# Gates of a linear recurrence in quarters of the array, its elementwise work spread and moved to VectorE, the last norm on rows of tokens

## What is computed

```
xc = causal_dwconv(x_rnn, conv_w, conv_b)            # 1280 channels, 4 taps
r = sigmoid(xb @ w_a + b_a)                          # w_a, w_x: 20 blocks of 64 x 64
i = sigmoid(xb @ w_x + b_x)
log_a = -8 * r * softplus(-lru_param)
a, mult = exp(log_a), sqrt(-expm1(2 * log_a))        # a = 0, mult = 1 where position == 0
h[t] = a[t] * h[t-1] + mult[t] * i[t] * xc[t]        # over the 512 tokens
...
x = x + gate1 * (merged @ w_out)
x = x + gate2 * ((silu(u_gate) * u_val) @ w_down)
return rmsnorm(x, final_g)                           # over the 1024 channels of each token
```

## Time and profile before

| | |
|---|---|
| median of three runs | 1829.65 us |
| the profiled execution's own time | 1828.8 us |
| its span, first to last instruction | 1827.0 us |
| PE busy | 1808.5 us (99%) |
| DVE busy | 1029.1 us (56%) |
| ACT busy | 754.9 us (41%) |
| POOL busy | 274.3 us (15%) |
| mean granted TensorE clock | 0.998 |

### The profile page before, as it was taken

The page is one execution under the profiler, slowest core; times in us unless marked ns, Lnnn a source line. Parts: engine busy times, 40 slices in busy tenths (PEclk is TensorE's granted clock), DMA queues, the critical chain, the costliest instruction groups (busy, mean ns, idle before and its releaser), DMA issues.

```text
span 1827.0 us, 21107 instructions
## 1 busy us (share of the span) xinstructions
PE 1808.5 (99%) x8268; PEld 1444.9 (79%) x8268; DVE 1029.1 (56%) x1522; ACT 754.9 (41%) x1197; POOL 274.3 (15%) x355
## 2 busy tenths in 40 slices
PE   9999999999999999999999999999999999999998
PEld 7888888878887888888887777766668888888886
DVE  8754554756566545554367587255544665435544
ACT  6554544425344222222344455355643344224431
POOL 4766536200000000000001120322110000000000
PEclk9999999999999999999999999999999999999999
DMA  6222222134235545553323222411133233323331
GB/s 213 95 84 87 70 87 90 59 114 150 93 132 179 190 150 184 191 192 96 126 81 99 92 76 76 138 64 58 35 132 122 70 98 99 92 93 92 97 99 59
DMA packets 64259, 198.92 MB, mean 109 GB/s; under 512 B 7136, under 2 KB 11488, under 8 KB 64160
## 3 DMA queue, kind: packets, MB, share of 16 engines
q1 hardware_dynamic: 64160, 197.57, 33.3%
HBM read 189.15 MB, written 8.39 MB: 108 GB/s over the span
## 4 chain that ended last, share of the span: by engine, by line
PE 71%; issue 21%; DVE 5%; ACT 1%; DMA 0%; POOL 0%; SPq 0%; POOLq 0%; DVEq 0%; ACTq 0%
PE bank L251 20%; PE bank L253 20%; PE bank L252 20%; PE bank L652 2%; DVE wlo L1396 1%; PE bank L682 1%; PE bank L667 1%; PE bank L544 1%; PE bank L297 1%; PE bank L340 1%; PE bank L356 1%; DVE tile L1932 1%; PE bank L386 0%; PE bank L377 0%; ACT whi L831 0%
## 5 line engine op out<-in xcount | busy, mean ns | idle before, releaser
L251 PE MATMUL bank<-tiler,whi 128*128 128x512 f32 x2260 | 909.1, 402 | 4.5 <-DVE tiler L1423 1.2
L253 PE MATMUL bank<-tiler,wlo 128*128 128x512 f32 x2260 | 891.8, 395 | 0.0
L252 PE MATMUL bank<-tiler,whi 128*128 128x512 f32 x2260 | 891.4, 394 | 0.0
L831 ACT ACTIVATE whi<-raw 128x1024 fp32r<-128x1024 f32 x284 | 298.8, 1054 | 559.1 <-PE bank L253 552.8
L251 PEld LDWEIGHTS bank<-tiler,whi 128*128 128x128 f32 x2260 | 426.1, 189 | 114.0 <-issue 14.5
L253 PEld LDWEIGHTS bank<-tiler,wlo 128*128 128x128 f32 x2260 | 425.5, 188 | 99.6
L252 PEld LDWEIGHTS bank<-tiler,whi 128*128 128x128 f32 x2260 | 426.1, 189 | 96.6 <-issue 3.3
L1396 DVE TENSOR_TENSOR wlo<-raw,whi 128x1024 fp32r<-128x1024 f32 x263 | 325.0, 1240 | 274.8 <-ACT whi L831 274.5
L2187 POOL TENSOR_TENSOR stat<-stat,scl 128x4 f32<-128x4 f32 x7 | 7.5, 1079 | 1120.3 <-DVE stat L1414 693.1
L2126 DVE SCALAR_TENSOR_TENSOR tile<-bank,sm,tile 128x511 f32<-128x511 f32 x44 | 33.0, 750 | 97.9 <-ACT tile L1370 61.9
L2178 POOL TENSOR_TENSOR wlo<-raw,whi 128x1024 fp32r<-128x1024 f32 x21 | 49.8, 2372 | 211.0 <-ACT whi L831 211.0
(11 more groups left out here) (363 smaller groups left out, 1603.8 us busy)
## 6 DMA issues: line engine op xcount, KB each, us to landing
raw<-wst SPq DMA_DIRECT2D x284, 512.0 KB, 3.6
wide<-wadaT SPq DMA_DIRECT2D x48, 512.0 KB, 3.5
tile<-xT SPq DMA_DIRECT2D x16, 256.0 KB, 6.0
spare<-tile SPq DMA_DIRECT2D x16, 256.0 KB, 2.0
tile<-spare SPq DMA_DIRECT2D x16, 256.0 KB, 5.5
out<-tile SPq DMA_DIRECT2D x8, 256.0 KB, 2.0
tile<-gblk SPq DMA_DIRECT2D x5, 256.0 KB, 4.6
us<-tile SPq DMA_DIRECT2D x4, 256.0 KB, 2.0
```

The costliest lines, as they stand in the source:

```text
L251: e.matmul(bank, whi[:, o:o + 128], hi, start=start, stop=False)
L252: e.matmul(bank, whi[:, o:o + 128], lo, start=False, stop=False)
L253: e.matmul(bank, wlo[:, o:o + 128], hi, start=False, stop=stop).then_inc(*sig("blk", n))
L831: e.activation(whi[:, c % NHL * W:(c % NHL + 1) * W], raw[:, c % NRAW * W:(c % NRAW + 1) * W], ACT.Copy).then_inc(*sig("hi", c))
```

## The change

1. **Gates in quarters.** Each of the two products of `gate_rnn(i)` becomes two of 64 rows and 64 columns, so the blocks of zeros are no longer multiplied. The parts of `w_a` go straight (rows 0-63 to partitions 0-63 of `B[4]`, rows 64-127 to 64-127), those of `w_x` crosswise into `B[5]`, so that the four parts use the four quarters of the array. ACT reads `B[5]` back in two halves.
2. **The LRU's order.** Exponentials 0 to 4 at m = 10 and 5 to 9 at m = 14, roots at m = 15 and 16; `lru_in` for 0 to 4 at m = 11 to 13 and 5 to 9 at m = 15; `lru_x` for all ten on DVE, at m = 16 to 18; the scans at m = 18 to 21. POOL's five products are gone.
3. **The last norm on rows of tokens.** ACT also scales each `HS[m]` by the gain (`OG`, tiles 0 to 7), PE turns 128x128 pieces of them into banks 4 to 7 (first 512 channels) and 0 to 3 (last 512), ACT takes the root of the mean square and DVE its reciprocal, now one number per partition. DVE scales the four tiles of the first half, ACT the four of the second, and SP sends them in an order that alternates. POOL's power, the diagonal, the spread and the fillers are gone.

```diff
                 for c in range(2):
-                    o = i % 2 * 256 + c * 128
-                    e.matmul(B[4 + c], F(GW[i // 2])[:, o:o + 128], F(XC[i]), start=True, stop=True).then_inc(*sig("lru_g", i, c))
+                    for x in range(2):
+                        of, to = slice(64 * x, 64 * x + 64), slice(64 * (x ^ c), 64 * (x ^ c) + 64)
+                        o = i % 2 * 256 + c * 128 + 64 * x
+                        ins = e.matmul(B[4 + c][to, :], F(GW[i // 2])[of, o:o + 64], F(XC[i])[of, :], start=True, stop=True)
+                    ins.then_inc(*sig("lru_g", i, c))
...
-            busy(B[7], 5)
-            total2("fin", 64, B[6])
-            total3("fin", 66, B[6])
-            busy(B[7], 8)
-            spread("fin", 65, B[7])
+            def out_turn(half_, js, ms):
+                for j in js:
+                    if half_ and ms[0] == 4:
+                        e.wait_ge(*at("h_dn", 1, 4 + j))
+                        if j == 0:
+                            e.wait_ge(*at("root", "fin"))
+                    for m in ms:
+                        e.wait_ge(*at("gs", m))
+                        ins = e.transpose(B[(0 if half_ else 4) + j][:, m % 4 * 128:m % 4 * 128 + 128],
+                                          F(OG[m])[:, j * 128:(j + 1) * 128], ident[:, :])
+                    if ms[-1] % 4 == 3:
+                        ins.then_inc(*sig("otr", half_, j))
...
+            total2("fin", 64, sums_at)
+            out_turn(0, range(4), [0, 1])
+            total3("fin", 66, sums_at)
+            out_turn(0, range(4), [2, 3])
+            out_turn(1, range(4), [4, 5, 6, 7])
...
-                e.activation(F(XX[i]), B[5], ACT.Sigmoid, bias=col("bx", i)).then_inc(*sig("lru_i", i))
+                for x in range(2):
+                    to, of = slice(64 * x, 64 * x + 64), slice(64 - 64 * x, 128 - 64 * x)
+                    ins = e.activation(F(XX[i])[to, :], B[5][of, :], ACT.Sigmoid, bias=col("bx", i)[to, :])
+                ins.then_inc(*sig("lru_i", i))
...
-                if m == 14:
+                if m == 10:
                     for i in range(5):
                         lru_exp(i)
...
+            e.activation(st, B[0][:, 508:512], ACT.Sqrt, scale=1.0 / 1024, bias=scl[:, HALF + 1:HALF + 2]).then_inc(*sig("root", "fin"))
+            e.wait_ge(*at("inv", "fin"))
+            for j in range(4):
+                e.wait_ge(*at("otr", 1, j))
+                e.activation(F(OT[4 + j]), B[j], ACT.Copy, scale=stat[:, ST_F + j:ST_F + j + 1]).then_inc(*sig("fin_a", j))
...
-            for k in range(8):
-                e.scalar_tensor_tensor(out=F(HS[k]), in0=F(HS[k]), scalar=col("gf2", k), in1=B[7], op0=MUL, op1=MUL).then_inc(
-                    *sig("fin", k))
+            e.reciprocal(stat[:, ST_F:ST_F + 4], stat[:, ST_F:ST_F + 4]).then_inc(*sig("inv", "fin"))
+            e.wait_ge(*at("inv", "fin"))
+            for j in range(4):
+                e.wait_ge(*at("otr", 0, j))
+                e.tensor_scalar(F(OT[j]), B[4 + j], stat[:, ST_F + j:ST_F + j + 1], None, MUL).then_inc(*sig("fin", j))
...
-                if m == 18:
-                    for i in range(5, 10):
-                        e.wait_ge(*at("lru_b", i))
-                        e.wait_ge(*at("lru_q", i))
-                        e.tensor_tensor(F(XX[i]), F(XX[i]), F(XC[i]), MUL).then_inc(*sig("lru_x", i))
```

More of the change, by code:

```diff
@@ L150 @@
 ACTS2 = [(42 + 2 * m, 43 + 2 * m) for m in range(11)]
+OG, OT = range(0, 8), range(8, 16)
 CG, CU = (64, 65, 66), (67, 68, 69)
@@ L1463, in vector @@
             e.memset(ones[:, :], 1.0).then_inc(*sig("ones"))
+            e.memset(scl[:, HALF + 1:HALF + 2], 1e-6)
             e.memset(scl[:, HALF:HALF + 1], -0.5).then_inc(*sig("half"))
@@ L1961, in vector @@
                     add_up("nq", 2, 72, (30, 31))
+                if 11 <= m <= 13:
+                    for i in range(2 * (m - 11), min(2 * (m - 10), 5)):
+                        lru_in(i)
                 if m == 15:
-                    for i in range(5):
+                    for i in range(5, 10):
                         lru_in(i)
-                        if i == 0:
+                        if i == 5:
                             add_up("nk", 1, 73, (32, 33))
@@ L1968, in vector @@
                     rope_k()
-                    for i in range(5, 10):
-                        lru_in(i)
+                    for i in range(5):
+                        lru_x(i)
                 if m == 17:
@@ L1973, in vector @@
                     variance("nq", B[5], 384, ST_Q)
-                    lru_x(0)
+                    lru_x(5)
                     diagonal("nk", ST_K, 75)
-                    lru_x(1)
+                    lru_x(6)
                     diagonal("nq", ST_Q, 71)
+                    lru_x(7)
                 if m == 18:
-                    for i in range(2, 5):
+                    for i in range(8, 10):
                         lru_x(i)
+                    for i in range(2):
+                        lru_scan(i)
                 if m == 19:
                     latent("kl", 2, LAT[3:], "kg", B[6], KL)
-                    for i in range(5):
+                    for i in range(2, 5):
                         lru_scan(i)
@@ L1988, in vector @@
                     latent("ql", 3, LAT[:3], "qg", B[7], QL)
-                    for i in range(5, 10):
+                    for i in range(5, 8):
                         lru_scan(i)
-                        if i == 6:
-                            start_of("in2", 21)
                 if m == 21:
@@ L2379, in gpsimd @@
             prep(CB * NCHUNK)
-            root("fin", ST_F)
         def sync(e):
@@ L2492, in sync @@
             chunks(NCHUNK)
-            for k in range(8):
-                e.wait_ge(*at("fin", k))
-                e.dma_start(out[k], F(HS[k])).then_inc(*sig("io%d" % k, 1, by=16))
+            for k in (0, 1, 4, 2, 5, 3, 6, 7):
+                if k < 4:
+                    e.wait_ge(*at("fin", k))
+                else:
+                    e.wait_ge(*at("fin_a", k - 4))
+                e.dma_start(out[k % 4][:, k // 4 * 512:k // 4 * 512 + 512], F(OT[k])).then_inc(*sig("io%d" % k, 1, by=16))
             for k in range(8):
@@ L2611 @@
     wst = nc.dram_tensor("wst", (NCHUNK, 128, CB * 128), F32, kind="ExternalInput").ap()
-    out = nc.dram_tensor("out", (8, 128, T), F32, kind="ExternalOutput").ap()
+    out = nc.dram_tensor("out", (4, 128, 1024), F32, kind="ExternalOutput").ap()
     spare = nc.dram_tensor("spare", (8, 128, T), F32, kind="Internal").ap()
```

32 lines of the change are left out of this document (18 added, 14 removed).

## The result

| | before | after |
|---|---|---|
| median (range) | 1829.09 us (1828.51 to 1829.97, 4 runs) | 1816.78 us (1815.53 to 1818.01, 4 runs) |
| profiled execution | 1828.8 us, span 1827.0 | 1816.73 us, span 1814.9 |

The ratio is 0.9932, with a 95% interval of 0.9915 to 0.9949. A second set of five runs gave 1816.76 us and 0.9937 [0.9924, 0.9951]. The forecast was 1818.4 us; the medians differ by 12.3 us, and 11.2 had been forecast.

What follows compares the result with a forecast made beforehand. PE, busy 99% of the span, was taken to bound the kernel. Terms -5.0 - 3.5 + 0.1 - 2.8 = -11.2 us gave 1818.4 us, with a likeliest range of 1816 to 1821 and a whole range of 1815.5 to 1827.5.

Steps and rivals of the forecast that it cites:

- Gates, -5.0: Ten gate calls on PE: four quarters at once, a call 1.72 to 1.22 us, 5.0 us saved in all.
- rival (a): Gate calls: only two quarters run at a time, a call costs 2.08 us, time 1827.0; chance 0.14.
- (b): Gate calls: quarters run one after another, a call costs 3.80 us, time 1844.1; chance 0.08.
- The LRU's order, -3.5: PE's three waits for DVE and ACT in the crowded stretch go, 3.5 us back whole; bounds 0 and 3.8.
- bound of 3.8: Upper bound on the PE waits won back by the LRU's new order, forecast at 3.5 us.
- 9.3 covers 5.0 plus the 3.5 of waits: Crowded stretch: DVE has 9.3 us less, enough for PE arriving 5.0 us earlier plus its 3.5 us of waits.
- rival (d): Long DVE rows are not POOL's doing; DVE gets 1.7 us more work, waits grow by 6.7, 1828.5; chance 0.05.
- ACT at gate 9, +0.1: ACT's 12.5 us against PE's 12.2 before gate 9: on time or 0.3 late, charged 0.1 us.
- rival (c): ACT's table changes cost 1.38 us more each when both tables were recently used: 2.7 us at gate 9, 1821.2; chance 0.07.
- The end, -2.8: Last norm: first output DMA at +4.4 instead of +7.21, 2.8 us earlier, then 7.1 us to the span's end.
- upper bound of 3.1: Most the end was to gain, in us, with ACT's root taking 0.16 instead of 0.3.

Runs made afterwards that it cites:

- twice: Changed kernel with each whole gate call issued twice over; stretch from first gate to the second layer's latent product 141.45 us, from one execution.
- straight: Changed kernel with the two parts of w_x going straight, so only two quarters of the array are used; 1825.31 us, ratio 0.9981.
- order_only: Kernel before with only the LRU's new order and all its products with the root on DVE; 1824.79 us, ratio 0.9978.
- gates_only: Kernel before with only the gates in quarters; 1824.92 us, ratio 0.9975.
- pool_again: Changed kernel with lru_x for row tiles 5 to 9 back on POOL; 1816.94 us, ratio 0.9932.
- dve_scales: Changed kernel with all eight output tiles scaled on DVE and ACT's four gone; 1816.85 us, ratio 0.9929.
- best: Changed kernel with later exponentials, root on ACT and reciprocal on DVE earlier at the feed-forward norm, fewer fillers at two norms; 1817.91 us, ratio 0.9936.

## Why the prediction was right

**Gates, -5.0.** Measured alone -5.07. The call went from 1.72 or 1.73 to 1.24, where 1.22 had been put together from the earlier trace rows: 0.86 for the passes and 0.36 for entering and leaving. `twice` splits the measured call into 0.86 and 0.38. `straight` gives rival (a)'s 2.08 us when only two quarters are in use, and shows that it was the quarters that decided. Rivals (a) and (b) are out. (The kernel before has one more product on a part of the array than the text ahead of the prediction says: L418 takes 64 of the 128 rows, 12 times, one after another. It is no case of two row halves at once.)

By the Trainium skill (TensorEngine Tiling (Array Packing), Restrictions and Gotchas, Gotcha 1) different row tiles can't access one PSUM bank simultaneously. The trace disagrees for this form: in both `straight` and the changed kernel, two parts from different rows wrote bank 4 at once, each its own 64 partitions. Another page of the Trainium skill (PSUM — Partial Sum Buffer, PSUM bank collisions raise a hardware error) quotes the same rule for row tiles, but the errors that it reports for two row tiles are for writes into one bank and one quadrant (32 partitions) of it. With a rule that goes by bank and quadrant the trace agrees. Two row tiles on the same partitions of one bank were not tried.

**The LRU's order, -3.5.** Measured alone -3.98. The mechanism is as put; the size was 0.5 short and lies past the bound of 3.8 that was given. Beside `order_only`, PE lost 0.85 us at L293, 0.95 at the L251 of 1107.31 and 1.83 at L585, together 3.63 for the three waits that the profile names, and 0.35 at the L251 of 1100.77, behind another late low part. That fourth one, with 0.11 us of idle time, does not stand in the list of waits, and it is most of what was missing.

**What I held beside it and what fell.** The prediction let DVE's relief pay for an earlier PE ("9.3 covers 5.0 plus the 3.5 of waits"), and rival (d) let the waits grow by 6.7 us if it did not. `gates_only` disproves that step: the gates took 5 us less with no relief at all for DVE, and no wait grew. The 5.0 needed no cover. (d)'s first half falls too, by `pool_again`: the long rows are POOL's doing. The estimate of what they cost (5.4 us) came back as 5.3.

**ACT at gate 9, +0.1.** Measured +0.49. The rows had summed to 12.5 us for ACT against 12.2 for PE, and I took off overlaps of 0.1 a row. From the start of gate 7's sigmoid to the end of gate 8's ACT took 1034.03 - 1021.19 = 12.84 us. The term was mis-sized by 0.4, past the 0.3 named as its worst. That it offsets most of the 0.5 by which the one before was short is luck. Table loads took 1.28 us and the next instruction began 0.02 us or less behind, as in the earlier trace rows; rival (c) is out. The Trainium skill (ScalarE: Activation LUTs, What ACT_TABLE_LOAD costs) gives 2.66 us with a drain for each change of table; the trace disagrees here, with 1.28 us and no drain to be seen.

**The end, -2.8.** Measured -2.92. Step by step from the last L254: sums at +0.24 as said, root at +3.00 for 3.1 (2.9, and 0.2 until the sums are visible), lasting 0.26 for 0.3, reciprocal 0.18 for 0.2, first DMA +4.29 for 4.4. The upper bound of 3.1 does not follow from the root of 0.16 that it names, which gives 2.9 to 3.0; nothing hangs on it. Then 7.02 us for 7.1: `dve_scales` shows that the bytes and not the engines set it.

**What was not in the sum.** -0.43 us ahead of the first gate, where nothing was changed, and -0.13 in two other stretches. The 0.43 arise in the first 50 us, and at that place the thirteen profiles spread from 0.8 us earlier to 1.4 later than before: that part is chance. Forecast -11.2; measured -12.1 between the two profiled executions and -12.3 between the medians.

## What to carry to other kernels

Products whose weights are two 64x64 blocks on a diagonal are worth laying in four quarters, crosswise in a second bank, if the passes that fall away take more than the 0.38 us that a visit to the split array cost here. Put several such products into one visit, since the price is paid once for each. Where engines follow each other by one chunk, as here, a shortening ahead of a crowded stretch moved the whole crowd and was kept in full. So run a term alone before a cover is subtracted from it. And count what a stretch costs from the starts of its instructions: the waits named in the profile, with 0.17 us added to each, fell 0.5 us short of the 4.0 that the stretch gave back.

## What the runs showed of the hardware that was not expected

The clock is lost for a moment in every profile at the layer's input norm, where PE does one-column sums and fillers: it falls to half (1.2 GHz) some time after 947 us, for 3.4 us in ten of the profiles and for 6.8 in three (`straight`, `dve_scales`, `best`). From the same matmul near 932 us to the first gate the ten took 40.5 to 40.6 us, `straight` and `dve_scales` 42.2, and `best`, with 3 fillers for 10, 40.9. That is one part of why executions of one kernel differ by 1 to 3 us, and the profiles show two more. `best` lost 1.8 us ahead of the norm, with a stretch at half clock near 9 us. `gates_only` and `twice` lost 1.6 us evenly between about 560 and 950 us, at a granted clock of 1.00 and where nothing was changed; the cause is open, and it is why their first gates start at 974.3 us where eight others start at 972.0 to 973.1. `dve_scales` has the long stretch with all 10 fillers in place, so whether `best` had it for its 3 is open.

POOL and DVE lengthen each other at more places than the one predicted. In the changed kernel, POOL's product `i * xc` of row tile 9 and then DVE's rows at that time:

```profile
1038.93 1.74 POOL L2407 TENSOR_TENSOR tile<-tile 128x512 f32<-128x512 f32 x1 [3.55 <-ACT tile L1170]
```

```profile
1038.22 0.69 DVE L1956 SCALAR_TENSOR_TENSOR tile<-tile 128x512 f32<-128x512 f32 x1
1038.83 0.69 DVE L1955 TENSOR_TENSOR tile<-tile 128x512 f32<-128x512 f32 x1
1039.55 1.66 DVE L1956 SCALAR_TENSOR_TENSOR tile<-tile 128x512 f32<-128x512 f32 x1
```

The DVE rows that began ahead of POOL's, the last by 0.1 us, are at 0.69; the next, inside it, takes 1.66. Scans, diagonals, products and low parts all showed it, each nearly twice as long or more. POOL's own product takes 1.28 us where no DVE row lies beside it (at 1034.10), and 1.74 here. In `pool_again` a diagonal and then a product of POOL's took 1.77 and 1.74 us side by side, 0.69 and 1.28 alone; a low part and a product took 2.31 and 2.28, 1.22 and 1.28 alone. So each takes about as long as both together, less 0.2 us, as if they took turns; the turns themselves are not shown. Rows of DVE that read a PSUM bank and one tile are not touched: beside the products `i * xc` of row tiles 2 to 7 the convolution's (L1937) stay at 0.75 us, and POOL's at 1.30.
